# Finishing a decoder block: the order of the last round's sums and the layer-norm statistics

## What is computed

```python
x = layer_norm(alpha * x + mix, ln1_g[l], ln1_b[l])
ffn = hierarchical_moe(x, ...)            # 32 experts, two per token
x = layer_norm(alpha * x + ffn, ln2_g[l], ln2_b[l])
```

## Time and profile before

| | |
|---|---|
| median of three runs | 393.3 us |
| the profiled execution's own time | 392.8 us |
| its span, first to last instruction | 390.5 us |
| mean granted TensorE clock | 0.974 of full speed |
| TensorE / VectorE / ScalarE / GpSimd busy | 92% / 41% / 35% / 9% of the span |

### The profile page before, as it was taken

How to read it: one execution, slowest core, us unless ns; L and a number is a source line. 1 busy time by engine, 2 the same in 40 slices (tenths; PEclk the granted TensorE clock), 3 DMA queues, 4 the chain that set the end, 5 groups by cost and what they waited for, 6 DMA issues and landing times.

```text
span 390.5 us, 8013 instructions
## 1 busy us (share of the span) xinstructions
PE 360.0 (92%) x3331; PEld 284.8 (73%) x3331; DVE 160.3 (41%) x338; ACT 137.3 (35%) x239; POOL 35.1 (9%) x42
## 2 busy tenths in 40 slices
PE   7999999999999999999899999999499598299985
PEld 7999988999999999998757575757246356157632
DVE  3465579787465567365730303030310112011136
ACT  4563555655535444435623131313011213012012
POOL 3310000000000000001000005209520000000001
PEclk9999999999999999999999999999799899599999
DMA  8689884966758768699999999999999999999962
GB/s 288 212 271 388 310 305 161 347 215 217 271 179 303 259 190 307 203 417 414 414 376 428 426 425 424 424 424 426 429 421 406 427 427 424 426 425 426 412 244 111
DMA packets 52054, 132.81 MB, mean 340 GB/s; under 512 B 2818, under 2 KB 36626, under 8 KB 41012
## 3 DMA queue, kind: packets, MB, share of 16 engines
q1 hardware_dynamic: 51572, 131.88, 87.1%
q0 software_dynamic: 304, 0.17, 0.2%
q10 hardware_dynamic: 144, 0.26, 0.2%
HBM read 131.25 MB, written 1.05 MB: 339 GB/s over the span
## 4 chain that ended last, share of the span: by engine, by line
PE 61%; DMA 20%; SPq 8%; DVE 7%; ACT 2%; issue 1%; DVEq 0%
PE bank L1179 15%; DMA gu<-in_w_up 14%; PE bank L1473 10%; PE bank L1208 7%; PE bank L1341 6%; PE bank L1509 5%; DMA raw<-in_w_in 5%; PE bank L1424 4%; PE bank L1521 4%; SPq L448 3%; PE bank L1211 3%; SPq L417 3%; DVE wl L813 3%; PE bank L1278 1%; ACT wh L631 1%
## 5 line engine op out<-in xcount | busy, mean ns | idle before, releaser
L813 DVE TENSOR_TENSOR wl<-raw,wh 128x1024 fp32r<-128x1024 f32 x54 | 65.9, 1224 | 55.2 <-ACT wh L631 55.2
L1473 PE MATMUL bank<-gu,xg 128*32 128x256 f32 x1024 | 63.3, 408 | 18.7 <-DMA gu<-in_w_up 18.1
L631 ACT ACTIVATE wh<-raw 128x1024 fp32r<-128x1024 f32 x54 | 56.6, 1056 | 61.2 <-DMA raw<-in_w_in 24.9
L1473 PEld LDWEIGHTS bank<-gu,xg 128*32 128x32 f32 x1024 | 33.7, 117 | 45.0 <-issue 25.2
L1208 PE MATMUL bank<-xh,wh 128*128 128x256 f32 x176 | 44.2, 289 | 0.1
L1208 PE MATMUL bank<-xl,wh 128*128 128x256 f32 x176 | 43.1, 283 | 0.0
L1208 PEld LDWEIGHTS bank<-xh,wh 128*128 128x128 f32 x176 | 33.6, 191 | 2.3 <-issue 2.0
L1077 DVE TENSOR_SCALAR xg<-bank,gcol,bcol 128x128 f32<-128x128 f32 x32 | 10.9, 406 | 59.0 <-PE bank L1424 59.0
L1208 PEld LDWEIGHTS bank<-xl,wh 128*128 128x128 f32 x176 | 33.6, 191 | 0.0
L1424 PEld LDWEIGHTS bank<-pick,x1p 128*128 128x128 f32 x256 | 29.8, 192 | 1.9 <-issue 0.9
L1424 PE MATMUL bank<-pick,x1p 128*128 128x128 f32 x256 | 30.2, 276 | 0.6 <-DVE pick L1048 0.6
(11 more groups left out here) (235 smaller groups left out, 587.1 us busy)
## 6 DMA issues: line engine op xcount, KB each, us to landing
gu<-in_w_up SPq DMA_DIRECT2D x31, 1024.0 KB, 20.0
gu<-in_w_gate SPq DMA_DIRECT2D x30, 1024.0 KB, 14.9
dn<-in_w_down SPq DMA_DIRECT2D x26, 1024.0 KB, 17.8
raw<-in_w_in SPq DMA_DIRECT2D x40, 512.0 KB, 4.8
raw<-in_w_o SPq DMA_DIRECT2D x8, 512.0 KB, 4.5
raw<-in_w_out_conv SPq DMA_DIRECT2D x4, 512.0 KB, 3.9
raw<-in_w_out_attn SPq DMA_DIRECT2D x4, 512.0 KB, 4.9
gu<-in_w_gate SPq DMA_DIRECT2D x1, 2048.0 KB, 10.5
```

The lines of the kernel that those rows point to most:

```text
L631: act.activation(wh[:, s, :].rearrange("p (k c) -> p k c", k=KC), raw[:, pair % NRAW, :].rearrange("p (k c) -> p k c", k=KC) [:, :, n % 2 ...
L813: dve.tensor_tensor(wl[:, s, :].rearrange("p (k c) -> p k c", k=KC), raw[:, pair % NRAW, :].rearrange("p (k c) -> p k c", k=KC) [:, :, n % ...
L1473: mm = pe.matmul(bank[6 - part][g, 0:DE], xg[:, k, g], w[:, e, part, k, :], start=(k == 0), stop=(k == KC - 1), skip_group_check=True)
```

## The change

The statistics tile gets room for four sets a tile of tokens instead of two. In the last round TensorE adds piece 1 into both tiles first, then piece 2 into both. Statistics are taken over 256 columns at a time, four sets for each tile of tokens, and `bn_aggr` merges four sets. VectorE takes the four sets of both left halves, and `scaled`, before it copies piece 1. Because pieces 1 and 2 lie in the same PSUM bank, TensorE now waits on a new semaphore, `third_read`, until VectorE has read piece 1's columns of a tile before it adds piece 2 into that tile. In each earlier round VectorE issues an `engine_nop` that raises this semaphore by two, so that it counts rounds.

```diff
-        stats = sb("stats", [P, TT, 2, 6])
+        stats = sb("stats", [P, TT, 4, 6])
...
+        third_read = sem("third_read")
...
-            def variance(t):
+            def variance(t, parts):
 
-                link(dve.bn_aggr(moments[:, t, :], stats[:, t, :, :]))
+                link(dve.bn_aggr(moments[:, t, :], stats[:, t, 0:parts, :]))
                 dve.tensor_scalar(moments[:, t, 1:2], moments[:, t, 1:2], EPS, None,
                                   ALU.add).then_inc(moment_done, 1)
...
                 take_y(c)
+                dve.engine_nop().then_inc(third_read, TT)
                 take_gathered(c + 2)
...
+            def statistics(t, piece):
+
+                at = piece * SEQ
+                return dve.bn_stats(stats[:, t, piece, :], bank[2 * t + at // HALF][:, at % HALF:at % HALF + SEQ])
+
             dve.wait_ge(added, first + 1)
-            dve.bn_stats(stats[:, 0, 0, :], bank[0][:, :])
+            statistics(0, 0)
+            statistics(0, 1)
+            dve.wait_ge(added, first + TT)
+            statistics(1, 0)
+            statistics(1, 1)
+            dve.tensor_tensor(scaled, bank[0][:, :], lng[:, 0:HALF], ALU.mult).then_inc(scaled_done, 1)
             take_y(last)
-            dve.wait_ge(added, first + TT)
-            dve.bn_stats(stats[:, 1, 0, :], bank[2][:, :])
-            dve.tensor_tensor(scaled, bank[0][:, :], lng[:, 0:HALF], ALU.mult).then_inc(scaled_done, 1)
             for t in range(TT):
-                dve.wait_ge(added, first + TT + (NY - 1) * (t + 1))
-                link(dve.bn_stats(stats[:, t, 1, :], bank[2 * t + 1][:, :]))
-                variance(t)
+                dve.wait_ge(added, first + TT + t + 1)
+                statistics(t, 2).then_inc(third_read, 1)
+            for t in range(TT):
+                dve.wait_ge(added, first + 2 * TT + t + 1)
+                link(statistics(t, 3))
+                variance(t, 4)
...
                             down(2, [1])
+                            scatter(1)
                             for t in range(TT):
-                                scatter(1, [t])
+                                pe.wait_ge(third_read, TT * c + t + 1)
                                 scatter(2, [t])
```

More of the change, by code:

```diff
@@ L968, in _ @@
                 link(dve.bn_stats(stats[:, t, 1, :], x1[:, t, HALF:DM]))
-                variance(t)
+                variance(t, 2)
             dve.wait_ge(x1T_ps, 4)
```

## The result

The changed kernel is **slower**: 395.97 us median against 393.35 on the same chip, ratio 1.0068 with a 95% interval of 1.0038 to 1.0099. The forecast was 393.8 in a range from 392.6 to 395.2, with 0.84 on no change that can be measured. Where the 2.6 us went is seen by reading the two traces in stages. The profiled executions have spans of 393.0 and 390.5 us.

A forecast was written before the change was run, and what follows sets the result against it. Bound: TensorE and weight transfers, DMA saturated from 230 to 372 us; the change works only on the end. The profiled 392.8 plus 0.5 is 393.3; standing 0.5 below the median, that gives 393.8 us, range 392.6 to 395.2.

The forecast's parts named there:

- The rest: Outside the end's chain: seven `engine_nop`s covered by VectorE's waiting, no DMA added, nothing counted for the 96-byte shift.
- the rivals: Alternative outcomes: TensorE's stop hidden, 393.3 us (0.12); instructions not fitting ahead of the copy, 395.2 (0.06); 96-byte shift, about 398 (0.06).
- The rival's price: Weight stream: shifted 8 KB runs need 33 transfers of 256 bytes, not 32; 4.4 us over 142 us; chance 0.06.
- The steps of the end: After the last down product: VectorE and left-half path times worked out step by step, end 0.5 us later.
- Statistics of tile 0: VectorE's last statistics of tile 0: fourth quarter starts 0.86 us later, behind TensorE's wait and reordered scatters.
- The price of a quarter: VectorE statistics over 256 columns instead of 512: 0.43 us each, bounds 0.35 and 0.70.
- First `rstd`: GpSimd's `rstd` of tile 0, after its epsilon: 0.60 us later, at 382.95.
- The five passes: VectorE's passes over half tiles after both tiles' statistics and epsilon: start 0.34 us later, at 383.71.
- ScalarE's output issue: Output issue at the end of the left-half path: 0.60 us later, at 387.61.
- The end: End of the kernel after the output issues and landing: 0.5 us later, forecast band +0.3 to +0.8.
- The copy: VectorE's copy of piece 1: starts at 379.48 as before, released by the down product, 0.18 us to spare.
- The five instructions: Four left quarter statistics and `scaled`, ahead of the copy: covered by idle time, VectorE free at about 379.30.

The follow-up runs named there:

- e1_shift96: Kernel before with an unused tile of 96 bytes a partition declared behind the statistics tile: 396.89 us against 392.81, ratio 1.0102.
- e2_home: Changed kernel with its statistics tile back at 96 bytes and the eight sets in free scratch of a weight buffer: 392.84 us against 392.81, ratio 1.0001.
- e5_shift128: Kernel before with an unused tile of 128 bytes behind the statistics tile: 396.69 us against 392.69, ratio 1.0099.
- e8_shift96_part: Kernel before with 96 unused bytes behind `gu0`, so `dn`, `gu1` and what follows are shifted: 394.58 us against 392.69, ratio 1.0049.
- e9_shift96_small: Kernel before with 96 unused bytes behind `gu1`, so only the tiles behind it are shifted: 393.27 us against 392.91, ratio 1.0011.
- e11_left_only: Kernel before with both left statistics (over 512 columns) and `scaled` ahead of the copy of piece 1, old scatter order: 392.58 us, ratio 0.9981.
- e10_order_only: Kernel before with the changed order of the scatters alone, old statistics over 512 columns, no wait on VectorE: 393.17 us against 392.91, ratio 1.0005.

## Why the prediction was wrong, point by point

**The step that failed** is in "The rest": "The larger `stats` tile shifts every tile behind it by 96 bytes; I count nothing for it". It measured 4.1 us alone (`e1_shift96`), and without it the change measured nothing (`e2_home`). That mechanism stood among the rivals, with its place, its point of decision (0.8% more time per run), its price (4.4 us) and a chance of 0.06; the range left it out. Two things were wrong there:

- *The evidence against it did not bear on it.* `dn_x` at 128 past a multiple of 256 and its 6.2 us against 6.8 were taken as a hint that such an offset is free. `dn_x` itself may well have been free, but that says nothing of the stream: `e5_shift128` has just that offset on the streamed tiles, at 1.0099. One transfer, timed from issue to landing among others, cannot show 1.5%: `dn_o`, aligned like `dn_z`, took 7.6 us in the same list. Why the packets of `dn_x` do not stand out in the trace (191 of the 205 packets of 8 KB that start from 190 to 200 us before take 309 ns) was not tried and stays open, as with `dn` behind `gu0` in `e8_shift96_part`.
- *The rival's price was near by luck.* One 256-byte transfer more in 32 would be 3% of a packet, and 1.5% was measured; but it was counted over 142 us only. From 180 us on the DMA engines are occupied throughout (share 1.01 from 180 to 230 us, too), and 1.5% of the 192 us to 372 is, as an estimate, some 2.8 us by the last weights. The profiles bear that out: `hs` starts at 373.33 to 375.37 us (mean 374.2) in the seven profiles with all three large weight tiles shifted, and at 370.08 to 373.29 (mean 371.6) in the five with `gu0`, `dn` and `gu1` at home. Part of the rest comes at the end, where the last piece of down weights is late: from `hs` to the end `e1_shift96` takes 19.6 us, the kernel before 18.76 and `e9_shift96_small` 19.19, none with a change there.

What the Trainium skill says of this ("DMA: Bandwidth & Descriptors", how a descriptor splits into AXI transactions) was set aside because it speaks of reads. Here the write side moved, the HBM side did not, and the cost came; so the measurement goes further than that page of the skill. By an estimate in the 32-byte beats of that page, an offset of 32 would cost a third of what 96 costs; measured, it costs no less (315.1 and 314.1 ns).

**The steps of the end were right.** They are read in `e2_home`, which has the change without the shift, counted from the copy of piece 1 and against the kernel before. The timeline of DVE of `e2_home`:

```profile
377.79 0.42 DVE L1118 COPY ys<-bank 128x256 f32<-128x256 f32 x1
379.01 0.86 DVE L1141 BATCH_NORM_STATS2 gu<-bank 128x6 f32<-128x256 f32 x2 [0.79 <-PE bank L1534]
380.23 0.43 DVE L1141 BATCH_NORM_STATS2 gu<-bank 128x6 f32<-128x256 f32 x1 [0.36 <-PE bank L1534]
380.70 0.26 DVE L959 BATCH_NORM_AGGREGATE moments<-gu 128x2 f32<-128x24 f32 x1
...
382.05 0.75 DVE L1162 SCALAR_TENSOR_TENSOR gu<-bank,moments,lng 128x512 f32<-128x512 f32 x1
```

The timeline of its PEld:

```profile
379.49 0.73 PEld L1534 LDWEIGHTS bank<-ys,put 128*128 128x128 f32 x4 [0.49 <-DVE gu L1141]
```

The timeline of its POOL:

```profile
381.24 0.60 POOL L617 TENSOR_TENSOR rstd<-moments,half_neg 128x1 f32<-128x1 f32 x1 [89.93 <-DVE moments L960]
```

And the timeline of its ACT queue:

```profile
385.90 0.39 ACTq L798 DMA_DIRECT2D out<-gu  x1
```

- *Statistics of tile 0:* forecast 0.86 us later. Measured 380.23 - 377.79 = 2.44 against 1.65: **0.79**. TensorE went on at 379.49, 0.05 after the third quarter (379.01 + 0.43), not 0.12. The place from which 0.12 was read may not have shown the price of two waits: TensorE still had a bias product in hand there (383.08 + 0.59).
- *The price of a quarter,* 0.43, was right; the merge of four sets took 0.26 us, 0.05 more than that of two, where 0.01 was set.
- *First `rstd`:* forecast 0.60 later. 381.24 - 377.79 = 3.45 against 2.87: **0.58**. *The five passes:* forecast 0.34. 4.26 against 3.89: **0.37**. *ScalarE's output issue:* forecast 0.60. 8.11 against 7.53: **0.58**.
- *The end:* forecast 0.5; 11.72 us from the copy against 11.05, **0.67**, inside the bounds of 0.3 to 0.8. How much of it the change makes is not shown: `e9_shift96_small`, with no change there, takes 11.33, `e11_left_only` 11.46 and `e10_order_only` 11.71.
- *The copy* still starts when the down product ends, with 0.11 us to spare instead of 0.18. The five instructions fit. By the formula of the Trainium skill ("VectorE: DVE Perf Modes", TRN2 errata), two quarters were estimated to take 0.13 us more than a half. Back to back in `e2_home`, from 375.47 to 376.23 us, two took 0.76 against 0.70, 0.06 more, and idle time covered that. That page of the Trainium skill gives its advice of 512 elements for SBUF sources; these statistics read PSUM.
- *The `engine_nop`* cost nothing that can be seen: `e2_home` has all seven.

Of the forecast's 0.5 us, the time of `e2_home` (1.0001, up to 1.0021) shows neither presence nor absence.

## What to carry to other kernels

A tile that grows moves every tile declared behind it: before costing the instructions of a change, work out where the DMA targets come to lie, and where a stream is saturated keep them on multiples of 256 bytes, which was enough here, by padding or by putting the new data into scratch that is free by then. A wait that is shorter at the end gains nothing if what it waits for is ordered behind more work: the last statistics here were halved, but of a tile completed 0.79 us later. And a single transfer's time from issue to landing can't refute an effect of 1%; the rate of a long stretch can.

## What the runs showed of the hardware that was not expected

The start of a DMA target in SBUF matters to a saturated stream of 8 KB packets from HBM: on a multiple of 256 bytes a packet took 309 ns in the median and the stretch ran at 423 GB/s; 32, 64, 96 or 128 bytes past one it took 312 or 313 ns (mean 314 to 315) and ran at 418 or 419. How far past made little difference. It is no rule for each transfer by itself: in `e8_shift96_part` shifted `dn` transfers kept to 309 ns behind `gu0` at home. What makes the packets longer (more transactions on the write side, or partly filled ones) the runs don't tell.
